# The end of the HGRN stage: another order of work in the last two heads, and a first output tile built from its high halves

## The reference

```python
proj = (h @ w_in).astype(jnp.float32)
q, fl, iv, g = jnp.split(proj, 4, axis=-1)
f = lb + (1.0 - lb) * jax.nn.sigmoid(fl)
k = 1.0 - f
...
# per block: decayed scores between tokens, output from scores and state, new state
scores = jnp.einsum('bhtk,bhsk,bhtsk->bhts', qc, kc, decay)
o = einsum(scores, ic) + einsum(qc * exp(bcum), s)
s = exp(b_last) * s + einsum(kc * exp(b_last - bcum), ic)
...
o = o * lax.rsqrt(jnp.mean(o * o, axis=-1, keepdims=True) + EPS)
o = o.reshape(bsz, t, D_MODEL) * norm_w.astype(jnp.float32) * jax.nn.silu(g)
return o.astype(h.dtype) @ w_o, s_fin.astype(s0.dtype)
```

## Time and profile before

| | us |
|---|---|
| median of three runs | 2769.44 |
| profiled execution | 2769.23 |
| its span in the trace | 2767.4 |
| around the span | 1.8 |
| TensorE busy | 2687.4 |
| VectorE busy | 2135.3 |
| GpSimd busy | 1273.7 |
| ScalarE busy | 841.1 |

### The profile page before, as it was taken

How to read it: one execution, slowest core, us unless ns; L and a number is a source line. 1 busy time by engine, 2 the same in 40 slices (tenths; PEclk the granted TensorE clock), 3 DMA queues, 4 the chain that set the end, 5 groups by cost and what they waited for, 6 DMA issues and landing times.

```text
span 2767.4 us, 41980 instructions
## 1 busy us (share of the span) xinstructions
PE 2687.4 (97%) x17508; PEld 2644.1 (96%) x17508; DVE 2135.3 (77%) x2389; ACT 841.1 (30%) x1259; POOL 1273.7 (46%) x913
## 2 busy tenths in 40 slices
PE   8999998999999999999999999889899999999998
PEld 8999898999999999999999999889899999999998
DVE  8996768999999855566777677786899999985555
ACT  3001534444444300031222122132444444430002
POOL 5222366777777532362121212115677777752324
PEclk9999999999999999999999999999999999999999
DMA  5221142212222522221111111104222222243222
GB/s 155 55 63 35 33 152 92 72 72 72 72 72 72 189 95 82 91 107 46 47 40 47 48 40 47 40 25 148 72 75 79 78 80 74 72 165 99 91 95 77
DMA packets 132365, 219.09 MB, mean 79 GB/s; under 512 B 67536, under 2 KB 85968, under 8 KB 132176
## 3 DMA queue, kind: packets, MB, share of 16 engines
q1 hardware_dynamic: 50928, 121.91, 13.3%
q10 hardware_dynamic: 81248, 94.49, 10.2%
HBM read 164.52 MB, written 51.86 MB: 78 GB/s over the span
## 4 chain that ended last, share of the span: by engine, by line
PE 86%; DVE 9%; POOL 2%; issue 1%; ACT 1%; DMA 0%; DVEq 0%; ACTq 0%; SPq 0%; POOLq 0%
PE BANKS L935 34%; PE BANKS L895 26%; PE BANKS L1201 13%; PE BANKS L1445 3%; PE BANKS L1022 2%; PE BANKS L1257 2%; DVE BANKS L2187 1%; PE BANKS L1245 1%; PE BANKS L1163 1%; POOL OPS L761 1%; DVE HGA L2617 1%; DVE HGA L2760 1%; DVE XL L2099 1%; PE BANKS L1302 1%; PE BANKS L1312 1%
## 5 line engine op out<-in xcount | busy, mean ns | idle before, releaser
L731 POOL TENSOR_TENSOR SMALL<-WRAW 128x1 f32<-128x1 f32 x108 | 30.2, 280 | 1108.9 <-PE BANKS L895 521.5
L935 PE MATMUL BANKS<-XB_A,OPS 128*128 128x288 f32 x3432 | 515.0, 298 | 20.3 <-issue 19.3
L935 PEld LDWEIGHTS BANKS<-XB_A,OPS 128*128 128x128 f32 x3432 | 477.3, 190 | 25.2 <-issue 22.4
L935 PE MATMUL BANKS<-XB_B,OPS 128*128 128x288 f32 x2904 | 437.4, 296 | 0.0
L895 PE MATMUL BANKS<-GHL,WH 128*128 128x384 f32 x2100 | 422.0, 335 | 6.2 <-POOL WL L734 3.4
L935 PEld LDWEIGHTS BANKS<-XB_B,OPS 128*128 128x128 f32 x2904 | 405.1, 189 | 0.1
L2325 DVE TENSOR_TENSOR X<-BANKS,X 128x1152 f32<-128x1152 f32 x152 | 206.2, 1356 | 239.0 <-PE BANKS L895 210.9
L895 PEld LDWEIGHTS BANKS<-GHL,WH 128*128 128x128 f32 x2100 | 369.9, 188 | 7.6 <-issue 3.8
L2510 DVE SCALAR_TENSOR_TENSOR C<-U,HGA,C 128x1168 f32<-128x1168 f32 x176 | 274.2, 1577 | 35.7 <-ACT C L1821 34.1
L734 POOL TENSOR_TENSOR WL<-WRAW,WH 128x1024 fp32r<-128x1024 f32 x108 | 269.0, 2491 | 8.7
L761 POOL TENSOR_TENSOR OPS<-TMP,OPS 128x512 fp32r<-128x512 f32 x176 | 236.8, 1356 | 63.1 <-ACT OPS L1745 63.1
(11 more groups left out here) (288 smaller groups left out, 5008.2 us busy)
## 6 DMA issues: line engine op xcount, KB each, us to landing
WRAW<-in_w SPq DMA_DIRECT2D x100, 512.0 KB, 3.4
RAW<-in_w SPq DMA_DIRECT2D x88, 512.0 KB, 4.3
GR<-g_kept ACTq DMA_DIRECT2D x22, 1152.0 KB, 5.3
g_kept<-C ACTq DMA_DIRECT2D x44, 512.0 KB, 2.6
x_kept<-X ACTq DMA_DIRECT2D x24, 576.0 KB, 2.7
XB_BF<-x_kept SPq DMA_DIRECT2D x16, 576.0 KB, 7.4
X<-in_x SPq DMA_DIRECT2D x8, 576.0 KB, 9.1
X<-in_x ACTq DMA_DIRECT2D x8, 576.0 KB, 7.5
```

The costliest lines, as they stand in the source:

```text
L935: ins = nc.tensor.matmul(out[:, cols], w[:, a, p, :], x[:, b, cols], start=s in OPENS and p == 0 and q == 0, stop=p == PAIRS - 1 and q == ...
```

## The change

Four things are moved or split; nothing is computed that was not computed before.

1. VectorE, heads 1 to 7: `inverse(h-1, 1)` stands between `own(h)` and `first_level(h)`, and no longer behind the copies of join 2. In head 6, `inverse(5, 2)` goes behind the drain of F, and `normed(5)` behind the copies of join 6.
2. VectorE, head 7 has an order of its own: the gate of head 6 ahead of the copies of 4A, the last reciprocal between these and the raising for join 6, G's drain ahead of that of join 6, raising for the keys ahead of the copies of 6A, and `stream_values`, `normed(6)`, three low halves behind. `gated(6)` now comes before the norm; before, it came behind it.
3. TensorE: tile 0 of the output projection is cut in `first_out` into products with XH, which need only ScalarE's rounding, and products with XL. The first stand between join 6, keys, states and outputs; the second stand behind. Tile 1 is no longer interleaved with piece 7 of tile 0 at its fifth piece but at its last.
4. ScalarE: four roundings stand ahead of the keys' copy; the gate's Silu and the others behind it; the last head's state output goes behind the last root.

```diff
@@ TensorE, head 7 @@
             joined(6, "A", h)
             joined(6, "B", h)
+            def first_out(k0, k1, highs=True, lows=True):
+                u = U_WO
+                s = u % 2
+                if k0 == 0 and highs:
+                    pe.wait_ge(w_split, u + 1)
+                    emptied_big(pe, "G", HEADS - 1)
+                for k in range(k0, k1):
+                    wh, wl = WH[:, s, k * P:(k + 1) * P], WL[:, s, k * P:(k + 1) * P]
+                    if highs:
+                        pe.wait_ge(x_hi, P_WO + k + 1)
+                        for q, w in enumerate((wh, wl)):
+                            for c in range(NCH):
+                                nc.tensor.matmul(ps_bank(T_HG, c), w, XH[:, k, third(c)], start=(k == 0 and q == 0),
+                                                 stop=False, skip_group_check=True)
+                    if lows:
+                        pe.wait_ge(x_lo, P_WO + k + 1)
+                        for c in range(NCH):
+                            ins = nc.tensor.matmul(ps_bank(T_HG, c), wh, XL[:, k, third(c)], start=False,
+                                                   stop=k == KD - 1, skip_group_check=True)
+                if k1 == KD:
+                    ins.then_inc(ps_full, 1)
+            first_out(0, 3, lows=False)
             keys(h)
+            first_out(3, 4, lows=False)
             state_steps(h)
             stream_states(h)
+            first_out(4, 6, lows=False)
+            outputs(h)
+            first_out(0, 1, highs=False)
+            sums(h)
+            first_out(1, 6, highs=False)
+            first_out(6, KD - 1)
...
-            projected(0, 0, 2)
-            outputs(h)
-            projected(0, 2, 4)
-            sums(h)
-            projected(0, 4, KD - 1)
-            projected(1, 0, 5)
-            projected(0, KD - 1, KD)
-            projected(1, 5, KD)
+            projected(1, 0, KD - 1)
+            first_out(KD - 1, KD)
+            projected(1, KD - 1, KD)
             for m in range(2, KD):
                 projected(m, 0, KD)
@@ ScalarE @@
                 widened(6, h)
                 if h + 1 < HEADS:
                     sigmoid_f(h + 1)
+                else:
+                    full_big(act, "G", h)
+                    for k in range(4):
+                        output_high(k)
                 tokens("KT", h, KT)
-                if h == HEADS - 1:
-                    for k in range(2):
+                if h < HEADS - 1:
+                    states_out(h)
+                else:
+                    for k in range(4, HEADS - 2):
                         output_high(k)
                     gate_of(h)
-                    for k in range(2, HEADS - 1):
-                        output_high(k)
-                states_out(h)
+                    output_high(HEADS - 2)
                 output_of(h)
                 if h + 1 < HEADS:
                     load_state(h + 1)
             root(HEADS - 1)
+            states_out(HEADS - 1)
             output_high(HEADS - 1)
@@ VectorE @@
                 own(h)
+                if h:
+                    inverse(h - 1, 1)
                 first_level(h)
...
+                if h == HEADS - 2:
+                    inverse(h - 1, 2)
                 picks(6, "A", h)
                 joined_raised(6, h)
                 picks(6, "B", h)
...
+            h = HEADS - 1
+            dc.inc(gated(h - 1))
+            picks(4, "A", h)
+            inverse(h - 1, 2)
+            joined_raised(4, h)
+            picks(4, "B", h)
+            projected("G", h, GATE)
+            joined_raised(6, h)
+            picks(6, "A", h)
+            picks(6, "B", h)
+            stream_values(h)
+            states(h)
+            normed(h - 1)
+            for k in range(3):
+                output_low(k)
+            stream_states(h)
+            for k in range(3, HEADS - 1):
                 output_low(k)
             dc.inc(gated(HEADS - 1))
-            output_low(HEADS - 2)
```

## The result

The changed kernel takes 2757.03 us (median of five, 2752.8 to 2759.43), against 2769.44 for the kernel before in the same set: a ratio of 0.9945, with an interval of 0.9935 to 0.9956. It is faster by 0.55%, inside the range of 2748 to 2759, and 4.7 us above the 2752.3 that was forecast.

What follows compares the result with a forecast made beforehand. TensorE, busy 97%, was taken as the bound, so gains come from its idle time and half clock in the last two heads. Head 6's 8.9 plus head 7's 8.1 us make 17.0, giving 2752.3 us, range 2748 to 2759.

Steps and rivals of the forecast that it cites:

- one of the signs that I had named for being wrong: Last two heads: the prediction is wrong if the clock still falls there; it claimed a granted clock of 1.0.
- Heads 1 to 5: VectorE's reciprocal, moved ahead of `first_level`, falls into an idle 2.43 us; cost 0 there, 0.1 us in head 6.
- Head 6: Join 6A follows F without a wait (6.48 us gained) and runs at full clock; 8.9 us gained in all.
- Head 7 up to the sums: Join 6A waits 0.5 us instead of 4.86, keys start at 1838.0 instead of 1842.95, sums at 1853.4.
- The priced meeting: Head 7: GpSimd's split can hold line 2700's second instruction for 0.8 us and the raising for the keys by 0.4.
- The sums and the low thirds: Head 7, after a wait of about 1.9 us: sums and their changeovers take 2.2 us, five low thirds 2.6.
- the clock falls in head 7 all the same: Rival, chance 0.13: the clock falls in one of head 7's waits of 1.7 to 2.4 us, giving back 2 to 5.
- The releaser of the sums: Head 7: sums wait about 1.9 us for VectorE's stream states (1853.0) and ScalarE's output copy (1853.2).
- Tile 2: Output tile 2 waits 2.4 us for GpSimd's split of unit 2 and starts 8.1 us earlier on the old clock.
- The residual: Rival, chance 0.05: residual lands late, tile 0's bank is free at 1884.3, head 7 gains nothing; time 2760.3 us.
- The late reciprocal: Rival, chance 0.03: the moved reciprocal isn't hidden in heads 1 to 5, costing 2.5 us in each; time 2764.7.
- half clock throughout: Rival, chance 0.02: TensorE stays at half clock from join 6A to output tile 2, 15 us slower; time 2784.

Runs made afterwards that it cites:

- x9: Changed kernel with the second reciprocal of heads 1 to 5 put back behind the copies of join 2; ratio 0.9953 to the kernel before.
- x4: Kernel before the change, with two of GpSimd's splits held until VectorE has raised the keys of the same head; ratio 0.9979 to the kernel before.
- x5: Changed kernel with the low products of pieces 1 and 2 of tile 0 moved ahead of head 7's sums; ratio 0.9934 to the kernel before.
- x1: Changed kernel with VectorE's order of head 6 as it was before; ratio 0.9987 to the kernel before.
- x3: Changed kernel with all six XH products of tile 0 behind the stream states, none in the earlier gaps; ratio 0.9974 to the kernel before.
- x6: Changed kernel with tile 0's last piece one piece of tile 1 earlier; ratio 0.9939 to the kernel before.
- x7: Changed kernel with GpSimd's split of output unit 1 held until VectorE has raised head 7's keys; ratio 0.9945 to the kernel before.
- x10: Changed kernel with head 7's two stream-state instructions right behind the states again, ahead of the norm and three low halves; ratio 0.9964 to the kernel before.
- x8: Changed kernel with the edits of x5, x6 and x7 together; 2752.84 us in the second set, ratios 0.9932 and 0.9941 to the kernel before.

## Why the prediction was right, and by what it missed

**What bounds it: right.** Idle time and half clock in the last two heads were the whole of it; the two halves, undone one by one, give all 15.3 us of the stretch. But one of the signs that I had named for being wrong did come: the clock still falls in head 7, once.

**Heads 1 to 5: right.** Taken at 0, measured at 0.21 (x9). TensorE has no new wait there: VectorE's drain makes it wait 12 times for 5.5 us in all, before and after. Join 2A of head 6, taken at 0.1, waits 1.24 after 1.13.

**Head 6: right, 9.1 for 8.9.** Join 6A without a wait, 1.79 for the forecast 1.86. Line 2695 took 0.68 at 1756.86, done well before the split began; x4 shows that the meeting was 2.9 of the 6.48 us.

**Head 7 up to the sums: right to 0.4.** Against the start of join 4A, forecast and measured starts were 9.8 and 9.94 for join 6A, 17.4 and 17.78 for the keys, 19.9 and 20.18 for the state steps, 32.8 and 33.22 for the sums. The priced meeting on the second instruction of line 2700 came exactly (0.84 for 0.8), and reached the keys as far as 0.6. The sum behind it has an unexplained 0.4: copies 4B and G's drain end at 1830.4 + 1.2 + 1.3 = 1832.9, and I wrote 1833.3, which with the named 0.4 makes up the 0.8. So the fit of the keys is in part luck; their wait was 0.93 where I had 1.7, since the work ahead of them ended 1.2 later than I had it and they themselves started only 0.4 later.

**The sums and the low thirds: the term that was mis-sized.** I had 2.2 for the sums and their changeovers and 2.6 for five low thirds, 4.8 together, taken from the old order, where they ran at full clock behind filled time. Measured were 6.10 (1846.81 to 1852.91), and 7.4 when the kernel ran again. In x5 the same work takes 5.0 (3.97, and 1.04 that had moved ahead). The step that failed is that I priced the wait before the sums, predicted at 1.9 and measured at 1.72, at its length alone: the clock falls in it or just behind it. This was the rival "the clock falls in head 7 all the same", at 0.13, to give back 2 to 5 us. It happened, at 1.1 in one profile and 2.4 in the other. In all eight profiles of versions that kept the wait of 1.71 to 1.72 (the two of the changed kernel, x1, x3, x6, x7, x9, x10) the sums took 3.07 to 3.62; in the three with 0.67 or 0.68 they took 1.88. The length of a wait alone doesn't decide it: in x4, join 6A of head 7 stood behind a wait of 1.86 and ran at full clock, in 1.89. So head 7 gave 6.2, or 4.9 in the second profile, where 8.1 was forecast. I had used the idle 1.13 before join 2A as the reason against it; the waits of 2.71 and 1.22 of the earlier trace rows were the nearer rows, and what I missed was to ask of each wait that I added what the clock does behind it.

**The releaser of the sums: half right.** I had named the new order on VectorE as the new wait, with ScalarE 0.2 behind. x10 shows that ScalarE alone makes the same wait.

**Tile 2: right.** 2.24 for 2.4, for GpSimd's split of unit 2, proven by x6.

**The total.** The stretch gained 15.3 where 17.0 was forecast: 0.2 more in head 6, 1.9 less in head 7. (Of that 1.9, 0.4 is the later start of the sums, 1.3 their length with the low thirds, and 0.2 lie behind that, where I let tile 0 end at 1872.0 though 1870.7 + 1.56 makes 1872.3.) The rest of the 4.7 us between 2752.3 and 2757.03 is 1.8 before the stage, 1.0 behind it and some 0.2 in heads 1 to 5, of which only the last surely belongs to the change. That the time lies inside the range is in part luck: in the other set the changed kernel gained 8.6 us (2769.78 to 2761.14) and not 12.4, and 2761.14 lies outside 2748 to 2759. Its profile there starts the stage 3.9 us later than the first one, in the same code, and loses 1.3 more in the stretch.

**The rivals.** The residual did not delay tile 0's bank (VectorE's add at 1867.22 waited for TensorE; only in x5 and in both profiles of x8 did it wait 1.1 to 1.3 us for the transfer, and was still done ahead of the split). The late reciprocal fell by x9, and half clock throughout by the granted 1.00 of head 6 and 0.97 of head 7.

## What to carry to other kernels

When a change cuts TensorE's idle time into new waits, price each of them twice: its length, and what the clock does to the work behind it; here the wait of 1.7 us before the sums cost another 1.1 to 2.4, the one of 2.24 before tile 2 another 1.5 in six profiles of eight, and one of 0.7 nothing. Work that needs only an early half of its input (here the products with the rounded part) is the right filler for them. Look also for instructions that VectorE can do in idle time instead of ahead of a critical run of short ones: three of them, moved, gave 9.1 of 15.3 us, with TensorE's list as it was.

## What the runs showed that I had not expected

**The same wait, different prices.** After the same wait of 1.71 or 1.72 the sums took 3.07 to 3.62, in one and the same kernel 3.09 and 3.62. The wait of 2.24 before tile 2 differs as much. In the first profile of the changed kernel the granted clock stays at 1.00 behind it. In x7 the first three matmuls already run at half clock:

```profile
1869.64 1.33 PE L1477 MATMUL BANKS<-XH,WH 128*128 128x384 f32 x3 [2.24 <-POOL WL L736]
```

In the second profile of the changed kernel the first three are still fast, and the clock falls less than 1 us behind them. Its timeline, and then a stretch of three us (the columns as above; the granted clock is 0.50):

```profile
1876.11 0.80 PE L1475 MATMUL BANKS<-XH,WH 128*128 128x384 f32 x3 [2.24 <-POOL WL L734]
1876.75 1.00 PE L1475 MATMUL BANKS<-XL,WH 128*128 128x384 f32 x3
```

```profile
1877.00:1880.00 3.00, 3.00 (x11) 3.00 (x10) 1.72 (x2) 2.29 (x3) 2.92 (x4) 0.50 1.00 278
```

Of the eight profiles with the wait of 2.24, the clock falls in or just behind the wait in six (x1, x3, x7, x9, x10 and the second of the changed kernel) and holds in two (the first of the changed kernel, and x5). The nine pieces behind the wait then take 15.6 to 15.8 us for 14.2. These 1.5 us lie behind the end of my stretch. With 0.72 or 0.73 before tile 2 (x6 and x8) the clock holds in all three profiles. The changed kernel's ten times span 9.5 us and the ten of x8 3.4; the clock can have a part in that, but the start of the HGRN stage alone moves by 7.6 us from profile to profile in code that is the same in all, so it isn't shown. The Trainium skill, "TensorE: Matmul & The Clock Gate", section "Part 1: The HAM clock gate", says that the gate's judging doesn't begin with the kernel, so that the same kernel meets it at another phase in each run. The two profiles of the changed kernel (sums of 3.09 and 3.62) fit that; no run here shows the phase itself.

**Where a blocking instruction falls decides its price.** Held back in x7, GpSimd's split blocked VectorE again, for 1.06 us (2.28 for 1.22) instead of 0.84; but behind that instruction VectorE would have waited anyway. The Trainium skill, "SBUF — State Buffer", section "Who interferes with whom", says that issue order decides who blocks. The rows of x7 agree: the split's last part had started at 1829.58, `stream_values` followed at 1830.76 and was the one to wait. And not every meeting blocks. In head 6 of the changed kernel the split's last part and a reciprocal, which reads one tile, ran beside each other, each at its usual length:

```profile
1760.82 2.40 POOL L734 TENSOR_TENSOR WL<-WRAW,WH 128x1024 fp32r<-128x1024 f32 x1
```

```profile
1761.11 2.54 DVE L2787 RECIPROCAL HGA<-HGA 128x384 f32<-128x384 f32 x1
```

The instructions that were stretched in these profiles include `joined_raised` and `stream_values`, with two inputs in SBUF. In x4 the split of unit 1, held to 1841.51, fell on copies and a drain out of PSUM, which kept their 1.22 and 1.35 us.
